# Attention that divides each probability tile by its row sums before it is turned, two turned-probability banks, and RMSNorm row scaling moved from GpSimd to VectorE

## The reference, cut to what matters

```python
def rmsnorm(x, g):
    y = x32 * lax.rsqrt(jnp.mean(x32 * x32, axis=-1, keepdims=True) + EPS)
    return (y * g.astype(jnp.float32)).astype(x.dtype)
...
    h = rmsnorm(x, g_mix_pre) * (1 + scale1) + shift1
    y, ctx_state = mixer(h)
    x = x + gate1 * rmsnorm(y, g_mix_post)
    h = rmsnorm(x, g_ffn_pre) * (1 + scale2) + shift2
    x = x + gate2 * rmsnorm(conv_ffn(h, ...), g_ffn_post)
```

```python
def softmax_logits(s, sink):
    ...
    e = jnp.exp(s - m)
    return e / (jnp.sum(e, axis=-1, keepdims=True) + jnp.exp(sink - m))
...
    o = einsum(p, v)
    y = concatenate([...]) @ w_out
```

## Time and profile before

| what | value |
|---|---|
| median of 3 runs (lowest to highest) | 1976.22 us (1975.79 to 1978.95) |
| the profiled execution's own time | 1974.18 us |
| its span, first to last instruction | 1972.2 us |
| mean granted TensorE clock | 0.945 |
| busy: PE, DVE, ACT, POOL | 1686.9 (86%), 1133.2 (57%), 731.8 (37%), 252.8 (13%) us |
| attention of layer 0, first scores to last copy into y | 136.5 us |
| division and first weight pair of the mix, layer 0 | 29.6 us |
| attention of layer 1 | 170.6 us |
| division and first weight pair of the mix, layer 1 | 39.4 us |
| reciprocal and eight chunks of the last post-norm | 23.4 us |

### The profile page before, as it was taken

How to read it: one execution, slowest core, us unless ns; L and a number is a source line. 1 busy time by engine, 2 the same in 40 slices (tenths; PEclk the granted TensorE clock), 3 DMA queues, 4 the chain that set the end, 5 groups by cost and what they waited for, 6 DMA issues and landing times.

```text
span 1972.2 us, 32385 instructions
## 1 busy us (share of the span) xinstructions
PE 1686.9 (86%) x11768; PEld 1547.0 (78%) x11768; DVE 1133.2 (57%) x1921; ACT 731.8 (37%) x1189; POOL 252.8 (13%) x199
## 2 busy tenths in 40 slices
PE   5697588793999999999769968776959999999994
PEld 1595466682999999999659965656849999999994
DVE  4585545566777767777763235553276662366524
ACT  3621355223544214442141136552346652244320
POOL 1451210004100000000150031310050000000003
PEclk9898799996999999999889989989979999999997
DMA  8251000150333443345322110000202222222211
GB/s 299 77 158 54 6 2 1 54 187 16 94 105 127 171 164 106 104 129 184 115 75 75 54 56 2 21 21 22 64 0 75 74 87 74 64 74 74 87 52 54
DMA packets 42797, 160.65 MB, mean 81 GB/s; under 512 B 5088, under 2 KB 6112, under 8 KB 42336
## 3 DMA queue, kind: packets, MB, share of 16 engines
q1 hardware_dynamic: 39888, 152.00, 23.5%
q0 software_dynamic: 1616, 6.68, 1.0%
q10 hardware_dynamic: 1216, 0.92, 0.2%
HBM read 156.04 MB, written 3.54 MB: 81 GB/s over the span
## 4 chain that ended last, share of the span: by engine, by line
PE 42%; DVE 5%; issue 2%; ACT 1%; POOL 0%; DVEq 0%; ACTq 0%; POOLq 0%
PE ps L1375 14%; PE ps L1376 14%; PE ps L1517 2%; PE ps L1547 2%; PE ps L1414 2%; DVE x L868 2%; PE ps L1532 1%; PE ps L1472 1%; PE ps L1473 1%; DVE work L847 1%; PE ps L1401 1%; PE ps L1427 1%; PE ps L1428 1%; PE ps L1587 1%; PE ps L1533 0%
## 5 line engine op out<-in xcount | busy, mean ns | idle before, releaser
L493 ACT ACTIVATE whi<-raw 128x1024 fp32r<-128x1024 f32 (+1 forms) x166 | 185.6, 1120 | 602.5 <-PE ps L1376 518.9
L1375 PE MATMUL ps<-hh,whi 128*128 128x320 f32 x920 | 288.6, 314 | 8.4 <-DVE wlo L777 8.4
L1376 PE MATMUL ps<-hl,whi 128*128 128x320 f32 x920 | 285.0, 310 | 0.0
L1376 PE MATMUL ps<-hh,whi 128*128 128x320 f32 x920 | 285.0, 310 | 0.0
L1375 PE MATMUL ps<-hh,wlo 128*128 128x320 f32 x920 | 285.0, 310 | 0.0
L1375 PE MATMUL ps<-hl,whi 128*128 128x320 f32 x920 | 284.9, 310 | 0.0
L1376 PE MATMUL ps<-hh,wlo 128*128 128x320 f32 x920 | 284.9, 310 | 0.0
L777 DVE TENSOR_TENSOR wlo<-raw,whi 128x1024 fp32r<-128x1024 f32 (+1 forms) x166 | 219.6, 1325 | 73.3 <-ACT whi L493 72.9
L1227 POOL TENSOR_TENSOR work<-y,work 128x640 f32<-128x640 f32 x32 | 59.7, 1870 | 1253.2 <-DVE work L847 1242.6
L1375 PEld LDWEIGHTS ps<-hh,whi 128*128 128x128 f32 x920 | 173.5, 189 | 10.6 <-DVE wlo L777 9.5
L1376 PEld LDWEIGHTS ps<-hh,whi 128*128 128x128 f32 x920 | 173.4, 189 | 1.1 <-issue 0.2
(11 more groups left out here) (211 smaller groups left out, 3599.2 us busy)
## 6 DMA issues: line engine op xcount, KB each, us to landing
raw<-in_w SPq DMA_DIRECT2D x134, 512.0 KB, 3.6
work<-in_wmodt SPq DMA_DIRECT2D x54, 512.0 KB, 3.6
raw<-in_w SPq DMA_DIRECT2D x32, 704.0 KB, 4.1
ring<-in_wmodt SPq DMA_DIRECT2D x26, 512.0 KB, 3.7
work<-in_wmod SPq DMA_DIRECT2D x16, 512.0 KB, 5.0
work<-in_rpb POOLq DMA_DIRECT2D x8, 480.0 KB, 4.4
x<-in_x SPq DMA_DIRECT2D x1, 2560.0 KB, 17.8
out_x<-x SPq DMA_DIRECT2D x8, 320.0 KB, 2.2
```

The costliest lines, as they stand in the source:

```text
L493: nc.scalar.activation(whi[:, s, 0:kk * P], raw[:, s, 0:kk * P], ACT.Copy).then_inc(s_hi, 1)
L1375: T.matmul(bankA[s], slot(w, s, k), h[:, k, 0:HT], start=st, stop=sp_)
L1376: last = T.matmul(bankB[s], slot(w, s, k), h[:, k, HT:NT], start=st, stop=sp_)
```

## The change

Three parts.

1. The division by the row sums moves into the attention loop. On DVE, `invert` takes the reciprocal of a unit's two row sums (for C after adding the sinks) when both exponents are done, and `divide` multiplies each head's probabilities by it in SBUF, in place; PE's `turn_probs` now waits for the divided ones (`s_pn`). `spread`, the multiply L1071, their two semaphores and the reciprocal over all sums are gone; `mix_in_lo` is eight `low`, `mix_pair` eight `pair_chunk`.
2. Head b's turned probabilities get a bank of their own (7), the context part of both heads lies side by side in bank 5 and is copied by one DVE instruction per unit; the values have bank 6 alone. PE's order becomes turn a(i), turn b(i), scores(i+2), values(i). DVE's order becomes invert and divide (i), take values (i-1), neg_max (i+1), copy turned (i).
3. `scale_rows` on POOL is gone. DVE scales the rows itself (`scale_row`), two ahead of their use.

The diff, cut:

```diff
+        turned_probs = [ps[:, 4, :], ps[:, 7, :]]
+        values_bank = ps[:, 6, :]
...
-                    nc.scalar.activation(pts[:, job.half, job.lo:NS], ps[:, 4, job.lo:NS],
+                    nc.scalar.activation(pts[:, job.half, job.lo:NS], turned_probs[job.half][:, job.lo:NS],
                                          ACT.Copy).then_inc(s_pta, 1)
...
                 for c in range(KD):
-                    scaled = 6 * layer + c - (1, -1)[layer]
-                    if layer or c > 1:
-                        act.wait_ge(s_os, scaled)
                     nc.scalar.activation(hh[:, c, :], y[:, c, :], ACT.Copy).then_inc(s_oth, 1)
...
+            def scale_row(n, src, k, s):
+                dve.wait_ge(s_rec, n + 1)
+                dve.wait_ge(s_tu, k + (8 * n + 1))
+                V.tensor_tensor(tn[s], chunk(src, k), rec, ALU.mult).then_inc(s_t, 1)
+
+            def rows_then(n, src, use):
+                for s in range(2):
+                    scale_row(n, src, s, s)
+                with dve.Fori(0, KD // 2 - 1) as h:
+                    for s in range(2):
+                        use(2 * h + s, s)
+                        scale_row(n, src, 2 * h + (s + 2), s)
+                for s in range(2):
+                    use(KD - 2 + s, s)
...
-            def copy_turned(job):
-                dve.wait_ge(s_pt, job.index + 1)
-                if job.unit:
-                    dve.wait_ge(s_o, job.unit)
-                V.tensor_copy(pts[:, job.half, NS:NT], ps[:, 5, 0:NP]).then_inc(s_ptb, 1)
+            def copy_turned(unit):
+                a, b = unit
+                dve.wait_ge(s_pt, b.index + 1)
+                if a.unit:
+                    dve.wait_ge(s_o, a.unit)
+                V.tensor_copy(pts[:, :, NS:NT], ps[:, 5, 0:2 * NP].rearrange("p (h n) -> p h n", h=2)).then_inc(s_ptb, 1)
+
+            def invert(unit):
+                a = unit[0]
+                own = sums[:, a.unit, :]
+                dve.wait_ge(s_p, a.index + 2)
+                if a.kind == "C":
+                    V.tensor_tensor(own, own, sinks[:, a.unit - 30, :], ALU.add).then_inc(s_den, 1)
+                    dve.wait_ge(s_den, a.unit - 30 + 1)
+                V.reciprocal(own, own).then_inc(s_rinv, 1)
+
+            def divide(job):
+                probs = pb[job.index % 4][:, job.lo:NT]
+                dve.wait_ge(s_rinv, job.unit + 1)
+                V.tensor_scalar(probs, probs, sums[:, job.unit, job.half:job.half + 1], None, ALU.mult).then_inc(s_pn, 1)
...
-                V.tensor_copy(y[:, a.chunk, a.q0:a.q0 + P], ps[:, 6 + a.unit % 2, 0:P]).then_inc(s_oe, 1)
+                V.tensor_copy(y[:, a.chunk, a.q0:a.q0 + P], values_bank[:, 0:P]).then_inc(s_oe, 1)
...
+                units = UNITS_OF[layer]
+                for job in units[0]:
+                    neg_max(job)
+                for i, unit in enumerate(units):
+                    invert(unit)
+                    for job in unit:
+                        divide(job)
+                    if i:
+                        take_values(units[i - 1])
+                    if i + 1 < len(units):
+                        for job in units[i + 1]:
+                            neg_max(job)
+                    copy_turned(unit)
+                take_values(units[-1])
...
-                    V.tensor_tensor(y[:, c, :], y[:, c, :], psf[:, at:at + NT], ALU.mult).then_inc(s_os, 1)
...
-                        G.tensor_tensor(tn[s], chunk(src, 2 * h + s), rec, ALU.mult).then_inc(s_t, 1)
...
-                pe.wait_ge(s_p, j + 1)
-                if j:
-                    pe.wait_ge(s_ptb, j)
+                pe.wait_ge(s_pn, j + 1)
+                if job.unit:
+                    pe.wait_ge(s_ptb, job.unit)
...
-                if a.unit >= 2:
-                    pe.wait_ge(s_oe, a.unit - 1)
+                if a.unit:
+                    pe.wait_ge(s_oe, a.unit)
...
-                scores(units[0])
+                for unit in units[0:2]:
+                    scores(unit)
                 for i, (a, b) in enumerate(units):
                     turn_probs(a)
-                    if i + 1 < len(units):
-                        scores(units[i + 1])
                     turn_probs(b)
+                    if i + 2 < len(units):
+                        scores(units[i + 2])
                     sum_values((a, b), v)
```

More of the change, by code:

```diff
@@ L852, in pre_norm, with low @@
                 reciprocal(n)
[L853 to L857, removed]
+                def low(k, s):
+                    dve.wait_ge(s_hh, k + (hidx + 1))
+                    V.tensor_tensor(chunk(hl, k), hf[s], chunk(hh, k).bitcast(F32), ALU.subtract).then_inc(s_hl, 1)
+                rows_then(n, x, low)
             def post_norm(layer, which):
@@ L862, in post_norm, with add @@
                 reciprocal(n)
[L863 to L871, removed]
+                def add(k, s):
+                    dve.wait_ge(s_t, k + (8 * n + 1))
+                    for st, f, t in SEG:
+                        xs = part(x, k, f, t - f)
+                        last = V.scalar_tensor_tensor(
+                            out=xs, in0=tn[s][:, f:t], scalar=coef[:, layer, st, which, bass.ds(k, 1)],
+                            in1=xs, op0=ALU.mult, op1=ALU.add)
+                    last.then_inc(s_tu, 1)
+                rows_then(n, y, add)
             dve.wait_ge(s_cst, 1)
@@ L1061, in low @@
                     V.tensor_tensor(hl[:, c, :], y[:, c, :], hh[:, c, :].bitcast(F32), ALU.subtract).then_inc(s_otl, 1)
-                first = 2 - 2 * layer
-                dve.wait_ge(s_oe, (30, 70)[layer])
-                for c in range(first):
+                for c in range(KD):
                     low(c)
[L1067 to L1070, removed]
-                    V.tensor_tensor(y[:, c, :], y[:, c, :], psf[:, at:at + NT], ALU.mult).then_inc(s_os, 1)
-                    if c > first:
-                        low(c - 1)
-                low(KD - 1)
             mix_in_lo(0)
@@ L1522, in turn_probs @@
             def turn_probs(job):
[L1524 to L1527 removed]
+                j, half = job.index, job.half
+                pe.wait_ge(s_pn, j + 1)
+                if job.unit:
+                    pe.wait_ge(s_ptb, job.unit)
                 if not job.prompt:
[L1529 to L1530 removed]
+                    if job.latent >= 2:
+                        pe.wait_ge(s_pta, job.latent - 1)
                     for c in range(job.lo, NS, P):
[L1532 to L1533 removed]
+                        T.transpose(turned_probs[half][:, c:c + P], pb[j % 4][:, c:c + P], ident[:, :])
+                T.transpose(ps[:, 5, half * P:(half + 1) * P], pb[j % 4][:, NS:NT], ident[:, :]).then_inc(s_pt, 1)
             def sum_values(unit, v):
                 a, b = unit
[L1538 to L1539 removed]
+                pe.wait_ge(s_ptb, a.unit + 1)
                 if not a.prompt:
                     pe.wait_ge(s_pta, b.latent + 1)
[L1542 to L1543 removed]
+                if a.unit:
+                    pe.wait_ge(s_oe, a.unit)
                 keys = [(a.lo + P * i, t) for i, t in enumerate(a.tiles)] + [(NS, a.vctx)]
@@ L1546, in sum_values @@
                     for job in unit:
-                        last = T.matmul(bank[job.rows, 0:P], v[:, t, job.v_col:job.v_col + DH], pts[:, job.half, c:c + P],
-                                        start=i == 0, stop=i == len(keys) - 1)
+                        last = T.matmul(values_bank[job.rows, 0:P], v[:, t, job.v_col:job.v_col + DH],
+                                        pts[:, job.half, c:c + P], start=i == 0, stop=i == len(keys) - 1)
                 last.then_inc(s_o, 1)
@@ L1574, in mix_pair @@
                 pe.wait_ge(s_fb, u0 + 2)
[L1575 to L1592, removed]
                 for k in range(KD):
```

13 lines of the change are left out of this document (1 added, 12 removed).

## The result

The changed kernel takes 1943.17 us (median of 4 runs, 1942.59 to 1944.44) where the kernel before, beside it, takes 1976.01: a ratio of 0.9836, 95% interval 0.9818 to 0.9853. The forecast was 1940, with a range of 1916 to 1968. The span fell from 1972.2 to 1940.6 us, by 31.6.

A forecast was written before the change was run, and what follows sets the result against it. No engine was full: handovers paced the mix, POOL the post-norms, and PE was what most attention units waited for. Mix -38.9, norms -25.6, attention +29 took 1974.2 to 1938.7, with 2 us added 1940; range 1916 to 1968.

The forecast's parts named there:

- Mix, -38.9: Mix stretches: 15.8 us each, saving 23.6 in layer 1, 13.8 in layer 0, plus 1.5 of layer 0's wait.
- The three parts of the lead into the first pair: Mix start: ACT's high part 0.7, DVE's low part 0.82, three handovers of 0.1, summed as 1.9 us.
- Norms, -25.6: DVE scaling rows instead of POOL: four post-norms save 4.7 us each (-18.8), four pre-norms 1.7 each (-6.8).
- -6.8 forecast: Four pre-norms, 1.7 us each: first row saves 1.1, low part falls from 1.36 to 0.82, later rows covered.
- Attention, +29: Both layers' attention: C's loop 5 or 13 with D's, POOL meetings 7, clock 4; summed 5 + 13 + 7 + 4.
- C's loop: Layer 1 attention, C units: chain through exponent, division, transposes and copy, 4.6 us against 3.78, 16 units, +13.
- D was given +5: Layer 1 attention, D units: second loop through the single values bank, 5.0 us, 0.3 over now, 16 latent units.
- 4.6 against 4.67: B and D units' exponent, division, transpose and copy loop, forecast against the present period; layer 0 stays as is.
- POOL's hold, +7: Layer 1's 64 latent-unit divides: chance 47 / 171 of meeting POOL, losing 0.3 to 0.5 us; bounds 0 to +18.
- the clock, +4: Attention around prompt units: longer round trips give more places of low PE clock; +4 us, bounds 0 and +25.
- The rival on the clock: Attention: PE's falling share in C lowers the clock and slows B, D and C units; +110, 2050 us, chance 0.08.
- the prediction's own signs of being wrong: Attention clock under 0.85, C period under 4.0 us, divides at 0.8, or mix chunks over 2.2 us.

The follow-up runs named there:

- the new order alone: Changed kernel without reciprocal, sink addition and division in the attention loop, its orders, banks and copies kept: 1894.65 us, ratio 0.9557.
- the early masks: Changed kernel with GpSimd's four mask subtractions moved ahead of its staging of the first C queries: 1937.63 us, ratio 0.9801.

## Why the prediction was right, point by point

The time (1940 for 1943) and the direction were right, and the mix, the post-norms and the attention as a whole by their own working. Inside the attention and in the pre-norms terms were mis-sized, and they cancel.

- **Mix, -38.9:** from the last copy into `y` to the next reciprocal layer 0 lost 16.3 us and layer 1 22.1, -38.3. The stretches that the sum names, with the wait, gave 11.9, 1.6 and 21.8, -35.3; some 3 us more came later in layer 0's mix, which the sum did not have. The order of the lists was the cost, as argued; the pairs run back to back. They took 17.6 us, not 15.8, since the clock falls among the first pairs: matmuls of 0.47 us for 0.31 from 1336.8 to 1340.0, a clock of 0.89 over the first 15.5 us where the earlier trace rows had 0.96 and 1.00. In the 8.2 us ahead of them PE is busy 4.7. (The three parts of the lead into the first pair add up to 1.8 and not to 1.9; measured it is 1.8.)
- **Norms, -25.6:** the four post-norms gave 4.7, 4.0, 4.2 and 4.3 us, -17.2 of the -18.8; a chunk takes 1.91 us and not 1.8. The pre-norms were **mis-sized**: -6.8 forecast, -4.2 measured (from their reciprocals to the first scores of the layer or the next reciprocal +0.1, -0.4, -1.1, -2.9). The last is not firm, since that stretch took 488.8 to 492.1 us in kernels with the change's norms. DVE's first low part fell from 1.36 to 0.82 as told, and in layer 1 PE's first matmul comes 4.3 us behind the reciprocal's end, where it was 5.9; of these 1.5 us 0.4 are left at the first scores. Where the rest goes was not followed. Another 1.3 us lies ahead of the first reciprocal, which starts at 61.7 to 68.7 us in the kernels here, so that it is not the change's.
- **Attention, +29:** measured +1.8 and +27.7, +29.5, with other parts. C's loop was given +13 and cost about 7, as above. A divide of 640 columns takes 0.55 us, 0.47 to the next start, for the 0.48 taken. D was given +5 and got 1.2 us shorter: of the units of two heads one does come 4.94 us behind the last, as the loop through the single values bank has it, but the next two come at 4.61 and 3.51 where 4.66 and 4.26 stood, the units around the prompt block are longer, and the end of the layer is 2.0 shorter. Layer 0 was given 0 by "4.6 against 4.67" and came out near it, by luck: the sum of a loop happened to equal the period of before, and hid that the new order alone is worth 13.6 us, which the division eats.
- **Of it POOL's hold, +7:** 4.4 us at the first unit by the early masks, about 5 in C's four held pairs, and some 4 in layer 0, where the prediction had no such term. Its mechanism was too mild: it took 0.3 to 0.5 us a meeting, though its own row (1.51 us for 0.42) had lost 1.1. A divide waits until the POOL instruction ahead of it has ended.
- **And the clock, +4:** the term that was furthest off. It cost 10.6 us in C. The rival on the clock named the right place and its cause, PE's falling share (more work on PE brought the clock back); it would have needed layer 0 too, which kept 0.94. Layer 1's 0.80 is one of the prediction's own signs of being wrong, a clock under 0.85; the other signs did not come (C's copies lie 4.76 us apart on the mean, the median divide of 640 columns takes 0.55, a mix chunk 2.0).

So the sum is right partly by luck: C's loop and D came out some 6 us each under the forecast, while the clock came out 6.6 over it, and the pre-norms, layer 0 and POOL's hold in layer 1 some 2 to 3 each.

## What to carry to other kernels

A division moved from the end into a loop costs what it adds to the longest chain of waits there, however short it is: here 50 us in the attention, with the half clock and POOL's holds that came with it; a reordering that lets the next unit's work stand between the division and its users won back as much. Compare a change against its own order without the new operation, not only against the kernel before, since two large terms may cancel. Where PE's share falls, read the granted clock of that stretch and price it.

## What the runs showed that was not expected

- A DVE multiply by a per-row scalar stands still until the POOL instruction that began ahead of it has ended: 4.41 us for a pair of 0.75, and 0.75 again with POOL's work moved. The two end at 1144.89 and 1147.17, the POOL subtractions that they wait for at 1144.68 and 1146.96. The Trainium skill, page "SBUF — State Buffer", section "SBUF: two separate sides", describes the port pair that the two engines share as held for a whole instruction, with the other fully blocked; these rows agree. A DVE addition of two columns beside it took 0.91 us for 0.16.
- Three useless matmuls per unit, 0.7 us of PE's time, raised the granted clock of C from 0.76 to 0.98 and shortened its stretch by 9.1 us.
